# Two merge-gate projections as one-level seven-product groups, with fill products and query turns placed anew

## The reference

```
z = h @ w_in                                # pool input | q | k,v of three branches | branch gates | merge gates
merge_g = sigmoid(z[..., OFF_MERGE_G:]).reshape(B, S, 2, D_MODEL)
y_pool = pool_mixer(u_pool, pool_w, pool_scale) @ w_pool_br
k_cmp, v_cmp = compress(k_c), compress(v_c) # gelu(flat @ w1 + b1) @ w2, 31 compressed rows
o = gc0 * softmax(q k_cmp) v_cmp + gc1 * (selected blocks) + gc2 * (window)
y_attn = o @ w_attn_br
x = x + (merge_g[:, :, 0] * y_pool + merge_g[:, :, 1] * y_attn) @ w_o
x = x + conv_ffn(rms_norm(x))
```

## Time and profile before

| | us |
|---|---|
| three runs | 1370.15, 1375.01, 1376.22 (median 1375.01) |
| the profiled execution | 1372.03 |
| its span in the trace | 1370.2 |
| mean granted TensorE clock | 0.996 |

### The profile page before, as it was taken

The page is one execution under the profiler, slowest core; times in us unless marked ns, Lnnn a source line. Parts: engine busy times, 40 slices in busy tenths (PEclk is TensorE's granted clock), DMA queues, the critical chain, the costliest instruction groups (busy, mean ns, idle before and its releaser), DMA issues.

```text
span 1370.2 us, 16139 instructions
## 1 busy us (share of the span) xinstructions
PE 1333.7 (97%) x5728; PEld 875.2 (64%) x5728; DVE 857.4 (63%) x2008; ACT 362.1 (26%) x891; POOL 264.3 (19%) x264
## 2 busy tenths in 40 slices
PE   4999999998999999999999999999999999999998
PEld 3444555544445446554455555888788888888887
DVE  5898999779240761133456676575667776777564
ACT  4223121145001002212456566121123333230000
POOL 1168568134011577300000000000000000000000
PEclk9999999999999999999999999999999999999999
DMA  9773425631230232102102002111232312314110
GB/s 321 188 132 131 124 56 152 221 125 62 92 110 3 95 89 86 68 0 93 63 0 63 1 1 62 62 62 47 64 121 62 123 62 82 103 62 169 63 69 31
DMA packets 89994, 120.58 MB, mean 88 GB/s; under 512 B 15448, under 2 KB 51614, under 8 KB 89916
## 3 DMA queue, kind: packets, MB, share of 16 engines
q1 hardware_dynamic: 85216, 110.81, 26.5%
q10 hardware_dynamic: 2956, 5.05, 1.2%
q0 software_dynamic: 1744, 3.70, 1.0%
HBM read 111.00 MB, written 6.84 MB: 86 GB/s over the span
## 4 chain that ended last, share of the span: by engine, by line
PE 92%; DVE 3%; ACT 2%; DMA 1%; issue 1%; POOL 0%; ACTq 0%; DVEq 0%; POOLq 0%
PE bank L1442 18%; PE bank L838 16%; PE bank L1468 9%; PE bank L851 8%; PE bank L1346 6%; PE bank L1317 6%; PE bank L873 5%; PE bank L1126 4%; PE bank L1297 3%; PE bank L1271 3%; PE bank L902 2%; PE bank L1171 2%; PE bank L1412 2%; PE bank L1253 1%; PE bank L1202 1%
## 5 line engine op out<-in xcount | busy, mean ns | idle before, releaser
L1442 PE MATMUL bank<-arena 128*128 128x256 f32 x1120 | 242.0, 379 | 0.0
L1442 PEld LDWEIGHTS bank<-arena 128*128 128x128 f32 x1120 | 212.7, 190 | 29.3 <-issue 0.4
L838 PE MATMUL bank<-arena 128*128 128x512 f32 (+1 forms) x544 | 230.9, 581 | 0.0
L838 PEld LDWEIGHTS bank<-arena 128*128 128x128 f32 x544 | 102.7, 192 | 113.5 <-issue 109.0
L1468 PE MATMUL bank<-arena 128*128 128x256 f32 x616 | 133.1, 379 | 0.0
L873 PEld LDWEIGHTS bank<-arena 128*128 128x128 f32 (+2 forms) x692 | 83.2, 144 | 75.8 <-issue 40.6
L1468 PEld LDWEIGHTS bank<-arena 128*128 128x128 f32 x616 | 117.0, 190 | 15.9
L873 PE MATMUL bank<-arena 128*128 128x128 f32 (+2 forms) x692 | 97.4, 279 | 22.4 <-ACT arena L1552 6.9
L851 PE MATMUL bank<-arena 128*128 128x512 f32 x256 | 113.5, 596 | 0.0
L2736 DVE CUSTOM_DVE_ANT_0 arena<-bank,arena 128x128 f32<-128x128 f32 (+3 forms) x128 | 57.7, 488 | 77.0 <-PE bank L1271 76.3
L1346 PE MATMUL bank<-arena 128*128 128x256 f32 x448 | 98.2, 380 | 0.6 <-DVE arena L2736 0.4
(11 more groups left out here) (370 smaller groups left out, 1855.0 us busy)
## 6 DMA issues: line engine op xcount, KB each, us to landing
arena<-in_w_in SPq DMA_DIRECT2D x14, 2048.0 KB, 7.9
arena<-in_w_up SPq DMA_DIRECT2D x20, 1024.0 KB, 6.9
arena<-in_w_ada SPq DMA_DIRECT2D x16, 512.0 KB, 8.9
arena<-in_w_down SPq DMA_DIRECT2D x8, 1024.0 KB, 7.4
arena<-in_w_out SPq DMA_DIRECT2D x2, 2048.0 KB, 9.7
arena<-in_w_attn_br SPq DMA_DIRECT2D x8, 512.0 KB, 7.8
arena<-in_w_o SPq DMA_DIRECT2D x2, 2048.0 KB, 8.0
rb_dram<-rb_one_dram ACTq DMA_DIRECT2D x1, 2560.0 KB
```

Source lines behind the costliest of these rows:

```text
L838: mm = pe.matmul(ps[:, 0:n], act[:, k, 128 * t:128 * t + 128], w[:, k, 0:n], start=(k == 0), stop=(k == kt - 1))
L1442: mm = pe.matmul(ps, left[:, k, :], right[:, k, :], start=(first and k == 0), stop=(k == 3), skip_group_check=True)
```

## The change

`m00` and `m01` become four groups of seven half products, one for each pair of row tiles and each half of the columns: group 0 is `m00` rows 0 and 1, group 1 `m00` rows 2 and 3, groups 2 and 3 the same of `m01`. DVE makes the sums of `hT` (once for both) and of the two weights; ACT copies P1, P5, P7 and P6 out of PSUM; DVE puts the blocks together in `mg`, and ACT takes the tanh there (`h_tanh`). The sums of `hT` and of `m00` stand on DVE behind the turn `kc` 3 and ahead of the hidden values. The eight query turns stand together. `kcm` and `vcm` follow group 0. The compressed scores, the groups and the `yp0` tiles are ordered anew, and with them the lists of ACT and DVE. In the loop the fill goes by pairs of units (even, odd), and P2 of the first `w_attn_br` group stands behind a turn and no longer ahead of it. The diff below is cut to its core: first the names of banks (P1, P2, P5, P7 of a group; P6 goes onto the bank of P1, P3 onto P5, P4 onto P7), then PE's list, ACT's list (from `h_copies(0, 0, 4)`, which stands behind the hidden tanh and the eight query copies), DVE's list, and PE's end of the loop. The functions added on ACT: `h_copies(g, n0, n1)` copies P1, P5, P7, P6 (numbers n0 to n1) of group g, `h_tanh(g)` takes the tanh of two rows of `mg` once `h_second(g)` is done.

```
+        PAIR_FILL = [(1, 3)] * 8 + [(1, 3), (1, 3), (0, 2), (0, 2)] * 2 + [(0, 2)] * 8 + [(0, 1)] * 8
+        per_sub = [m for pair in PAIR_FILL for m in pair]
-        per_sub = [(8, 6, 4, 2)[i] / 4 for i, _, _ in SUB2]
...
+        half_names(0, 0, 3, 1, 2)
+        half_names(1, 3, 2, 0, 1)
+        for j, b in enumerate((2, 3, 0, 1)):
+            proj_at(("ypm", j), b)
+        half_names(2, 2, 3, 0, 1)
+        proj_at(("yp0", 0), 3)
+        half_names(3, 0, 1, 3, 2)
+        for t, b in ((1, 2), (2, 1), (3, 0)):
+            proj_at(("yp0", t), b)
...
-            pe.wait_ge(qrope_done, TT)
+            pe.wait_ge(qrope_done, 2 * TT)
             for m in range(4):
                 turn(("qt2", m), [row2[:, t, 128 * m:128 * m + 128] for t in range(TT)])
-            one_rows("m00", 0, "m00", hT)
-            pe.wait_ge(qrope_done, 2 * TT)
             for m in range(4):
                 turn(("qt2", 4 + m), [q2b[:, t, 128 * m:128 * m + 128] for t in range(TT)])
-            one_rows("m00", 1, "m00", hT)
+            def h_products(g, *names):
...
+                    if name == "P5":
+                        pe.wait_ge(shsum_done, q + 1)
+                        pe.wait_ge(thsum_done, g // 2 + 1)
+                    if fresh:
+                        ps = begin_proj(("h", g, name))
+                    else:
+                        pe.wait_ge(hcopy_done, 4 * g + {"P6": 1, "P3": 2, "P4": 3}[name])
+                    for k in range(4):
+                        mm = pe.matmul(ps[:, 0:256], left[:, k, :], right[:, k, :], start=(fresh and k == 0), stop=(k == 3),
+                                       skip_group_check=True)
+            for m in range(4, 8):
+                aux_out(pe, ("qt2", m))
+            h_products(0, "P1", "P2", "P5", "P7", "P6", "P3", "P4")
...
-            one_rows("m00", 2, "m00", hT)
-            one_rows("m00", 3, "m00", hT)
+            h_products(1, "P1", "P2", "P5", "P7", "P6", "P3", "P4")
...
+            compressed_scores(0)
+            h_products(2, "P1", "P2", "P5", "P7")
+            compressed_scores(1)
+            h_products(2, "P6", "P3", "P4")
+            compressed_turn(0)
+            one_rows("yp0", 0, "yp0", ypT)
+            compressed_scores(2)
+            h_products(3, "P1", "P2", "P5", "P7")
+            compressed_turn(1)
+            compressed_scores(3)
+            h_products(3, "P6", "P3", "P4")
+            one_rows("yp0", 1, "yp0", ypT)
+            compressed_turn(2)
+            one_rows("yp0", 2, "yp0", ypT)
+            one_rows("yp0", 3, "yp0", ypT)
+            compressed_turn(3)
...
+            h_copies(0, 0, 4)
...
+            h_tanh(0)
+            h_copies(1, 0, 4)
...
+            h_tanh(1)
+            compressed_exp(0)
+            h_copies(2, 0, 3)
+            compressed_exp(1)
+            h_copies(2, 3, 4)
+            compressed_in(0)
+            h_tanh(2)
+            compressed_exp(2)
+            h_copies(3, 0, 3)
+            compressed_in(1)
+            compressed_exp(3)
+            h_copies(3, 3, 4)
+            h_tanh(3)
...
             step(v.memset(hid, 0.0))
+            aux_ready(v, ("kc", 3))
+            for q in range(2):
+                for part in range(4):
+                    row_part(hT, q, sH[q], part, shsum_done)          # 128 x 512 each
+            for part in range(4):
+                weight_part(weights(v, "m00"), tH[0], part, thsum_done)   # 128 x 1024 each
             for a in range(2):
                 aux_ready(v, ("hid", a))
...
+            def h_first(g):
+                v.wait_ge(hcopy_done, 4 * g + 1)
+                proj_ready(v, ("h", g, "P2"))
+                v.tensor_tensor(mg[:, 2 * q, c0:c0 + 256], c[0], pbank(("h", g, "P2"))[:, 0:256], ALU.add)\
+                    .then_inc(pfree(("h", g, "P2")), 1)
+                v.wait_ge(hcopy_done, 4 * g + 3)
+                step(v.tensor_tensor(c[2], c[2], c[1], ALU.add))
+            def h_second(g):
+                v.wait_ge(hcopy_done, 4 * g + 4)
+                v.tensor_tensor(mg[:, 2 * q + 1, c0 + 256:c0 + 512], c[3], c[2], ALU.add)
+                proj_ready(v, ("h", g, "P3"))
+                step(v.tensor_tensor(mg[:, 2 * q, c0 + 256:c0 + 512], c[3], pbank(("h", g, "P3"))[:, 0:256], ALU.add))
+                v.sem_inc(pfree(("h", g, "P3")), 1)
...
+                proj_ready(v, ("h", g, "P4"))
+                step(v.tensor_tensor(mg[:, 2 * q + 1, c0:c0 + 256], c[3], pbank(("h", g, "P4"))[:, 0:256], ALU.add))
+                v.sem_inc(pfree(("h", g, "P4")), 1)
...
+            h_first(0)
...
+            h_second(0)
+            v.wait_ge(pooled_done, 4)
+            for part in range(4):
+                weight_part(weights(v, "m01"), tH[1], part, thsum_done)
+            h_first(1)
+            h_second(1)
+            compressed_scores(0)
+            h_first(2)
+            compressed_scores(1)
+            compressed_out(0)
+            h_second(2)
+            gated(0)
+            compressed_scores(2)
+            h_first(3)
+            compressed_out(1)
+            compressed_scores(3)
+            h_second(3)
+            compressed_out(2)
+            gated(1)
+            compressed_out(3)
+            gated(2)
+            gated(3)
...
+                if 0 <= n - 2 < NS2:
+                    sub_turn(n - 2)
                 if n == NS2 + 1:
                     s_product(0, "P2")
-                if 0 <= n - 2 < NS2:
-                    sub_turn(n - 2)
```

More of the change, by code:

```diff
@@ L312, in program, with proj_at, half_names @@
         name_aux(*[("qt2", m) for m in range(8)], "kcm", "vcm")
[L313 to L323, removed]
+        HALVES = [("m00", 0), ("m00", 1), ("m01", 0), ("m01", 1)]
+        def proj_at(name, b):
+            PROJ[name], PBANK[name], PUSE[name] = len(PROJ), b, uses[b]
+            uses[b] += 1
+        def half_names(g, *banks):
+            for name, b in zip(("P1", "P2", "P5", "P7"), banks):
+                proj_at(("h", g, name), b)
+            for name, onto in (("P6", "P1"), ("P3", "P5"), ("P4", "P7")):
+                PROJ["h", g, name], PBANK["h", g, name] = len(PROJ), PBANK["h", g, onto]
+        half_names(0, 0, 3, 1, 2)
[7 more added lines that the diff above has]
+            proj_at(("yp0", t), b)
+        for name in (("cq", 0, 0), ("cq", 0, 1), ("cq", 1, 0), ("cq", 1, 1), ("cp", 0), ("cq", 2, 0), ("cq", 2, 1), ("cp", 1),
+                     ("cq", 3, 0), ("cq", 3, 1), ("cp", 2), ("cp", 3)):
+            name_aux(name)
         SUB2 = [(i, 2 * P + s, b) for i in range(TT) for P in range(4) for b in range(2) for s in range(2)]
@@ L446, in program @@
               [(0, 128, lambda: cmp_w1_2[0].rearrange("a (k p) n -> p (a k) n", p=128))])
[L447 to L448 removed]
+        wchunk("m00", ("h", 1, "P4"), w_in_2, KT, OFF_MG)
+        wchunk("m01", ("h", 3, "P4"), w_in_2, KT, OFF_MG + 512)
         wchunk("yp0", ("yp0", 3), w_pool_br_2, 4, 0)
@@ L1232, in _ @@
                     .then_inc(proj_done, 1)
[L1233 to L1238, removed]
             for m in range(8):
@@ L1246, in _, with compressed_scores, compressed_turn @@
             aux_out(pe, "vcm")
[L1247 to L1256, removed]
-                    fill2(("m01", i))
-                for tc in ((), (0,), (1,), (2, 3), ())[i]:
-                    pe.wait_ge(cnorm_done, tc + 1)
-                    turn(("cp", tc), [pc[:, tc % 2, 128 * b:128 * b + 128] for b in range(4)])
-                if i < TT:
-                    fill2(("yp0", i))
+            def compressed_scores(i):
+                for odd in range(2):
+                    r = slice(64 * odd, 64 * odd + 64)
+                    ps = begin_aux(("cq", i, odd))
+                    for h in range(odd, 16, 2):
+                        mm = pe.matmul(ps[:, 16 * (h - odd):16 * (h - odd) + NCMP],
+                                       qT2[r, h // 2, 128 * i:128 * i + 128], kcmp[r, h // 8, 0:NCMP],
+                                       start=True, stop=True)
+                    mm.then_inc(aux_done, 1)
+            def compressed_turn(i):
+                pe.wait_ge(cnorm_done, i + 1)
+                turn(("cp", i), [pc[:, i % 2, 128 * b:128 * b + 128] for b in range(4)])
+            compressed_scores(0)
[3 more added lines that the diff above has]
+            compressed_turn(0)
+            for j in range(4):
+                proj_out(pe, ("ypm", j))
+            one_rows("yp0", 0, "yp0", ypT)
[9 more added lines that the diff above has]
+            compressed_turn(3)
             def sub_scores(n):
@@ L2717, in compressed_out @@
                     .then_inc(cnorm_done, 1)
-            for i in range(TT + 1):
-                if i < TT:
-                    compressed_scores(i)
-                for tc in ((), (0,), (1,), (2, 3), ())[i]:
-                    compressed_out(tc)
-                if i < TT:
-                    gated("yp0", "m00", i, 0)
+            compressed_scores(0)
[14 more added lines that the diff above has]
+            gated(3)
```

135 lines of the change are left out of this document (87 added, 48 removed).

## The result

| | before | after |
|---|---|---|
| median of 10 runs each, us | 1371.03 | 1384.95 |
| lowest and highest | 1369.67, 1376.22 | 1377.24, 1389.02 |
| the profiled execution | 1372.03 | 1388.71 |
| its span | 1370.2 | 1386.8 |
| mean granted clock in it | 0.996 | 0.983 |

The ratio of the times is 1.0088, with a 95% interval of 1.0062 to 1.0114. The table's last row is where to begin: a clock of 0.983 over 1386.8 us is 47.2 us at half level, before it was 0.996 and some 11 us. The page's busy times don't show it: PE looks as busy as before, since a slow product counts as a busy one. The profiled execution is 3.8 us above the median of its kernel, so what is read from it is somewhat more than the typical case.

What follows compares the result with a forecast made beforehand. PE, busy 97% of the span, was taken to set the time; savings of products and loop, eaten by waits and clock, summed to +6.2 us, giving 1379.5 us (own range 1375 to 1384; with rivals 1372 to 1387).

Steps and rivals of the forecast that it cites:

- A: m00 and m01 products: 224 records at the seven-product pace replace 128 longer ones, -6.7 us (6.2 to 6.9).
- B: Before group 0: PE waits for query copies behind DVE's m00 sums and hidden values, +10.0 us (6.6 to 11.8).
- C: First products after the query-copy stall: clock at half level for 3.4 us, +1.7 us (0 to 3.4).
- D: P2 of group 1: waits for a bank DVE frees behind the vcm copies, +1.2 us (0.5 to 1.6).
- E: cp 1 turn behind P7 of group 3: PE waits for DVE's h_first(3) and compressed_out(1), +3.2 us (2.8 to 3.5).
- F: yp0 1: takes the bank of the just finished P4 of group 3, +0.5 us (0.3 to 0.8).
- G: Weights of yp1: PE's 0.4 us wait for their transfer goes, -0.4 us.
- I: Loop: waits for ACT's turn copies go, three of four bank 7 waits stay, -4.1 us (-5.6 to 0).
- H: Compressed scores: 2.5 clock falls, one sure at scores 3, where before two, +0.8 us (-3.3 to +3.3).
- Rival 2: Clock stays down twice as long after the first stall and falls in every score stretch: +10.4, 1384 us; chance 0.22.
- a sign of being wrong: DVE's four m00 sums: the prediction is wrong if they take under 1.5 us each.
- Rival 3: PE never waits, so only products, yp1 weights and loop count: -11.2, 1362 us; chance 0.08.

Runs made afterwards that it cites:

- split run: Changed kernel without its waits, with DVE's m00 sums 0 and 1 between the hidden tiles, 2 and 3 behind them: 1365.55 us, ratio 0.9945 to the kernel before.

## Why the prediction was partly right

1384.95 is inside the range of 1372 to 1387, and the sign that I gave 0.36 came true: slower by more than 0.5%, where my likeliest case was no change. The forecast's own range, 1375 to 1384, was missed by 1 us. As a difference the miss is larger. The forecast stood on 1373.3 (1379.5 less its 6.2), and the kernel before measured 1371.03: +13.9 stands against +6.2, and against +13.7 at the upper end of the range. That the time is inside owes something to luck with the base. Term by term, in the profiled executions:

| step | predicted | measured | how |
|---|---|---|---|
| A products | -6.7 | -6.6 | group 12.19 (563.32 to 575.51 in the split run), four 48.8; eight tiles 55.4 at 13.84 for two |
| B turns, sums | +10.0 | +9.1 | 559.52 - 546.94 - 3.5 |
| C clock behind it | +1.7 | 0.0 | 12.32 for 56 records, 12.35 at full clock in the split run; about 0.9 of B is clock |
| D | +1.2 | +1.4 | row at 575.88 |
| E | +3.2 | +3.1 | row at 634.62 |
| F | +0.5 | +0.7 | row at 650.58 |
| G and I, loop | -4.5 | -5.6 | 221.8 before, 216.2 after |
| H clock in the scores | +0.8 | +11.2 | 14.6 longer than at full clock, before 3.4 |
| fall at 60 us | | +2.7 | |
| sum | +6.2 | +16.0 | the spans differ by 16.6 |

Of the 16.0, 14.8 are clock (11.2, 2.7 and the 0.9 in B). The terms without the clock add up to +1.2, where I had +3.7.

- **Step H failed, by size.** I counted falls, 2.5 of them at the 1.7 us that those of before had cost, and wrote that `cp` 1's stall makes the last one sure. There were four, but four at 1.7 are only the +3.3 of my upper end; the other 7.9 us are length. The fall at `cp` 1 was 13.7 us long and cost 6.1 by itself (0.5 on the turn, 2.9 on the scores, 2.7 on P6, P3 and P4). Two of the three others were 6.8 us and not 3.4. Rival 2, "the clock, slower", named the mechanism; its +10.4 still took each fall in the scores at its old length, and got part of its sum from C, which didn't come. The fall of 13.7 us is in each of the three profiles that have the wait with scores 3 behind it, one of them of the kernel before, and in none of the eleven others; how the two make it stays open, as said above.
- **Step B was right for the most part.** DVE's sums took 6.1 us, between the 4.9 at their size and my 8.1. At 1.22, 1.50, 1.24 and 2.17 only the last was at the 2 us that I gave each, and two were under the 1.5 that I had named as a sign of being wrong. The first ran at its own 1.22 while POOL's stretched from 1.47 to 2.53, so it is POOL that was late there. I had charged DVE for every sum; the rows show it only for some. What I hadn't named is that turns 2 and 3 need the banks of `hid`, which DVE empties behind its sums (3.23 us ahead of turn 2). It cost nothing extra, as the copies of ACT come later anyway. The clock was down from 551.5 to 558.5, partly in B's idle time, where it costs nothing, and partly on the turns. ACT's eight copies began at 554.21 and would have ended at 558.3 at the 0.51 us of before; the last two waited for the slow turns, and they ended at 559.2. So about 0.9 us of B is clock, by this estimate. Group 0 was at full clock, so C was in the wrong place.
- **A, D, E, F and I came out within about 1 us.** The waits for ACT's copies of the turns are gone, three of ACT's four waits for bank 7 stay, as written.
- **Rival 3 is what the change could have been.** The split run has no wait, and without its clock it is 12.8 us shorter than the kernel before (1362.5 - 10.2 against 1370.2 - 5.1); the rival had -11.2. In the median 7.2 of it arrive.

What stays open: why falls behind the scores are sometimes 3.4 and sometimes 6.8 us. Every version with the seven products has 17 to 25.5 us at half clock without any wait at `cp` 1, the kernel before 10 to 12, and the closer order in eight products 18. The form of the products made no difference in the order of before, and spacing the scores didn't help; the runs don't settle more. Nor do they say why the clock fell in the wait at `cp` 1 and not in two waits of the same length elsewhere.

## What to carry to other kernels

Before moving work that covered another engine's chain, look for a piece of the new work that needs nothing from that chain, and put it in the gap (P1 and P2 between the turns, two sums between the hidden tiles). A wait of the tensor engine was dearest just ahead of narrow products: 2.9 us cost 6.8 there, and one of 2.2 us cost 3.6 with one dense tile in between, so look for a dense tile to put between the wait and the narrow products; one version of each was measured. And give a fall of the clock a wide range, not the price of those seen in a kernel without waits: here 1.7 us became 6.1.

## What the runs showed of the hardware

- The falls of the granted clock came in three lengths, 3.4, 6.8 and 13.7 us; the longest only when an idle time of about 3 us (2.9 to 3.1) stood right before a turn and 32 products of 31 columns. It began 2.0 to 2.6 us into that idle time.
- The length of the idle time alone doesn't say it: waits of 3.2 and 2.2 us with 1.6 us of turns between them had 6.8 us at half clock (in the changed kernel; 4.2 and 1.1 us did so in the run with `compressed_out(1)` first), one of 4.7 us between turns and 256-column products 3.4 us, 3.9 us in three pieces none, 2.2 us ahead of a dense tile none, and 2.9 us, twice, with no narrow products of 31 columns behind it, none.
- A fall can come with no idle time at all: behind 576 us the kernel before had no wait, and two of 3.4 us came at and behind 3.3 us of products of 31 columns.
- The Trainium skill ("TensorE: Matmul & The Clock Gate", section "HAM oscillation — how this bites in real kernels") has idle gaps of some us throw the array to half clock; those of its example are 3 to 5 us. The runs agree for the wait of 4.7 us and for that of 2.9 us at `cp` 1, and show none for one of 2.2 us and two of 2.9 us elsewhere.
- DVE's sums and POOL's operations stretch each other, and either may be the one to pay: sums of 1.22 to 2.28 us, POOL operations of 2.53 for 1.47. The Trainium skill ("SBUF — State Buffer", section "SBUF: two separate sides") has the two exclude each other, the one that starts first going ahead; the rows agree with the exclusion, and which of them is late differs from one pair to the next.
